# One hybrid decoder layer on one core: the cached-key products move to GpSimd, VectorE keeps one sum per page

## The reference, cut to what matters

```python
s_past = jnp.einsum('bthd,bshd->bhts', q, k_past) * scale
s_past = s_past + cq[..., None] + tail
p = softmax(concatenate([s_past, s_new]))
out = einsum('bhts,bshd->bthd', p[..., :P], v_past) + ...
```

## Time and profile before

| what | value |
|---|---|
| median of 3 runs | 1842.69 us (1839.71 to 1845.56) |
| profiled execution, from first to last instruction | 1838.9 us |
| TensorE busy | 1581.3 us (86%) |
| VectorE busy | 1037.4 us (56%) |
| ScalarE busy | 631.3 us (34%) |
| GpSimd busy | 242.0 us (13%) |
| mean granted TensorE clock | 0.908 |

### The profile page before, as it was taken

One profiled execution on the slowest core, in us unless ns is written; L12 is line 12 of the kernel. 1 busy time (PEld: TensorE's weight loads), 2 busy tenths in 40 slices (PEclk: granted clock), 3 DMA queues, 4 the chain that ended last, 5 costly groups with the idle time before them and its releaser, 6 DMA issues.

```text
span 1838.9 us, 33832 instructions
## 1 busy us (share of the span) xinstructions
PE 1581.3 (86%) x12263; PEld 1455.3 (79%) x12263; DVE 1037.4 (56%) x3203; ACT 631.3 (34%) x730; POOL 242.0 (13%) x379
## 2 busy tenths in 40 slices
PE   5999989783966667879777699999999999999996
PEld 4999868772743444569756699999999999999996
DVE  5557858567685887464663544444344444444444
ACT  5333313222241331333343344444233333333332
POOL 1000122121212222212103300000000000000332
PEclk9999989886977757789878799999999999999998
DMA  7456899886968688564342244554455554554553
GB/s 271 175 190 246 328 348 402 335 347 211 324 201 314 205 299 287 205 258 182 115 138 76 93 179 180 182 181 175 141 178 189 192 180 179 181 181 141 180 181 117
DMA packets 88612, 390.28 MB, mean 212 GB/s; under 512 B 9144, under 2 KB 22208, under 8 KB 66640
## 3 DMA queue, kind: packets, MB, share of 16 engines
q1 hardware_dynamic: 39824, 233.98, 35.4%
q0 software_dynamic: 39376, 143.15, 21.4%
q10 hardware_dynamic: 9328, 12.13, 1.9%
HBM read 379.13 MB, written 10.10 MB: 212 GB/s over the span
## 4 chain that ended last, share of the span: by engine, by line
PE 62%; DVE 14%; DMA 5%; issue 4%; ACT 2%; POOLq 1%; POOL 0%; DVEq 0%; ACTq 0%
PE bank L1388 18%; PE bank L1389 18%; PE bank L1390 18%; DVE page L933 4%; DMA page<-vc_dram 3%; DVE wlo L834 2%; DMA page<-kc_dram 2%; PE bank L1492 2%; ACT whi L492 1%; PE bank L1583 1%; DVE hl L873 1%; DMA g_s<-s_dram 1%; DMA nb<-mem_fm_dram 1%; DVE nb L888 1%; DVE g_dd L1099 0%
## 5 line engine op out<-in xcount | busy, mean ns | idle before, releaser
L1388 PE MATMUL bank<-hh,whi 128*128 128x264 f32 (+1 forms) x2688 | 779.3, 290 | 40.4 <-DVE hl L873 21.3
L1389 PE MATMUL bank<-hl,whi 128*128 128x264 f32 (+1 forms) x2688 | 770.9, 287 | 0.0
L1390 PE MATMUL bank<-hh,wlo 128*128 128x264 f32 (+1 forms) x2688 | 770.0, 286 | 0.0
L834 DVE TENSOR_TENSOR wlo<-raw,whi 128x2048 fp32r<-128x2048 f32 (+1 forms) x232 | 491.8, 2120 | 405.4 <-ACT whi L492 405.1
L492 ACT ACTIVATE whi<-raw 128x2048 fp32r<-128x2048 f32 (+1 forms) x232 | 410.4, 1769 | 837.8 <-PE bank L1390 833.7
L1388 PEld LDWEIGHTS bank<-hh,whi 128*128 128x128 f32 x2688 | 516.4, 192 | 55.0 <-issue 35.3
L1389 PEld LDWEIGHTS bank<-hl,whi 128*128 128x128 f32 x2688 | 517.0, 192 | 0.7 <-issue 0.7
L1390 PEld LDWEIGHTS bank<-hh,wlo 128*128 128x128 f32 x2688 | 514.1, 191 | 0.0
L933 DVE CUSTOM_DVE_ANT_0 page<-page,qb 128x128 f32<-128x128 f32 x1024 | 225.6, 285 | 70.8 <-DMA page<-kc_dram 52.4
L1388 PE MATMUL bank<-f_hi,whi 128*128 128x264 f32 x704 | 202.5, 288 | 7.5 <-DVE f_lo L1364 7.5
L1390 PE MATMUL bank<-f_hi,wlo 128*128 128x264 f32 x704 | 201.7, 287 | 0.0
(11 more groups left out here) (247 smaller groups left out, 1057.0 us busy)
## 6 DMA issues: line engine op xcount, KB each, us to landing
raw<-p_gu_dram SPq DMA_DIRECT2D x88, 1024.0 KB, 4.8
page<-kc_dram POOLq DMA_DIRECT2D x128, 512.0 KB, 6.2
page<-vc_dram POOLq DMA_DIRECT2D x128, 512.0 KB, 6.3
raw<-p_dn_dram SPq DMA_DIRECT2D x64, 704.0 KB, 4.1
raw<-p_fox_dram SPq DMA_DIRECT2D x24, 1024.0 KB, 4.8
raw<-p_gla_dram SPq DMA_DIRECT2D x24, 1024.0 KB, 7.7
raw<-p_out_dram SPq DMA_DIRECT2D x16, 1024.0 KB, 4.9
raw<-p_mem_dram SPq DMA_DIRECT2D x8, 1024.0 KB, 8.3
```

The source lines that it names most:

```text
L834: tt(wlo[:, k % 4, 0:blocks * P], raw[:, k % 4, 0:blocks * P], whi[:, k % 2, 0:blocks * P], ALU.subtract).then_inc(S("w_split"), 1)
L1388: mm(out, blk(whi, k % 2, b), rh, start=start, stop=False)
L1389: mm(out, blk(whi, k % 2, b), rl, start=False, stop=False)
L1390: return mm(out, blk(wlo, k, b), rh, start=False, stop=stop)
```

## The change

GpSimd now multiplies each key page in place with the query: `times_q` waits for the query and for the page, makes one `tensor_tensor` of 128x1024 and increments `k_mul`. It does so 7 items after it issued the page's load (`LAG`), ahead of the next fetch. The products of the last items of a turn thus come among the first fetches of the next. VectorE makes one `tensor_reduce` per page over all 8 heads (`k_sum`), one page later in its order than before, and frees the page with it. In the cross attention, `x_scores` becomes one product of 128x1024 and one sum, both on VectorE. `arrived` only moves.

```diff
@@ -359,6 +359,10 @@
             sp.wait_ge(S("y_out"), 64)
 
 
+        def arrived(t, q):
+
+            return 16 * (q // 8 + 1) if isinstance(t, int) and t == 0 else 64 * t - 32 + 16 * (q // 8 + 1)
+
         @block.gpsimd
         def _(pool):
             pool.dma_start(pts[:, :], io["pt_row"]).then_inc(S("pt_in"), 16)
@@ -374,10 +378,33 @@
                     pool.wait_ge(S(sem), value)
                 pool.dma_start(page[:, slot, :], io[src][ds(r * P, P), :]).then_inc(S(f"page_in{slot}"), 16)
 
+            LAG = 7
+
+            def times_q(t, j):
+
+                q = j if isinstance(t, int) and t == 0 else MIX.index(("k", j))
+                pg = page[:, q % SLOTS, :]
+                pool.wait_ge(S("q_b"), t + 1)
+                pool.wait_ge(S(f"page_in{q % SLOTS}"), arrived(t, q))
+                pool.tensor_tensor(pg, pg, qb[:, :], ALU.mult).then_inc(S("k_mul"), 1)
+
+            def times_before(t, q):
+
+                if q >= LAG:
+                    if MIX[q - LAG][0] == "k":
+                        times_q(t, MIX[q - LAG][1])
+                elif isinstance(t, int) and t == 1:
+                    times_q(0, 16 - LAG + q)
+                elif MIX[q + 32 - LAG][0] == "k":
+                    times_q(t - 1, MIX[q + 32 - LAG][1])
+
             pool.wait_ge(S("n_sq"), 4)
             for j in range(8):
+                if j >= LAG:
+                    times_q(0, j - LAG)
                 fetch("kc", j, j)
             for j in range(8, 16):
+                times_q(0, j - LAG)
                 fetch("kc", j, j - 8, "k_used", j - 7)
 
             def mixed(t, q):
@@ -393,11 +420,15 @@
                 fetch("kc" if now == "k" else "vc", 16 * t + j if now == "k" else 16 * t - 16 + j, q % SLOTS, sem, value)
 
             for q in range(32):
+                times_before(1, q)
                 mixed(1, q)
             with pool.Fori(2, 8) as t:
                 for q in range(32):
+                    times_before(t, q)
                     mixed(t, q)
             for j in range(16):
+                if j < LAG:
+                    times_before(8, j)
                 if j < SLOTS:
                     kind, i = MIX[32 - SLOTS + j]
                     fetch("vc", 112 + j, j, *(("k_used", 113 + i) if kind == "k" else ("v_used", 97 + i)))
@@ -437,10 +468,6 @@
                 cross_page(b)
             square_sums(3, "xo", "xo_go", 1)
             square_sums(4, "dn1", "n_lo_done", 16)
-
-        def arrived(t, q):
-
-            return 16 * (q // 8 + 1) if isinstance(t, int) and t == 0 else 64 * t - 32 + 16 * (q // 8 + 1)
 
         HN_BANKS = (2, 3, 6, 7)
 
@@ -923,19 +950,26 @@
 
             tail4 = tail[:, :].rearrange("p (h b j) -> p j b h", h=H, b=ND)
 
+            def k_slot(t, j):
+
+                q = j if isinstance(t, int) and t == 0 else MIX.index(("k", j))
+                return q, q % SLOTS
+
+            def k_sum(t, j):
+
+                _, slot = k_slot(t, j)
+                dve.wait_ge(S("k_mul"), 16 * t + j + 1)
+                dve.tensor_reduce(s_raw[:, j, :], page[:, slot, :].rearrange("p (h d) -> p h d", h=H), AX.X, ALU.add
+                                  ).then_inc(S("k_used"), 1)
+
             def k_page(t, j):
 
-                q = j if isinstance(t, int) and t == 0 else MIX.index(("k", j))
-                slot = q % SLOTS
-                dve.wait_ge(S(f"page_in{slot}"), arrived(t, q))
-                for h in range(H):
-                    pk = page[:, slot, P * h:P * h + P]
-                    ins = dve.tensor_tensor_reduce(out=pk, in0=pk, in1=qb[:, P * h:P * h + P], scale=1.0, scalar=0.0,
-                                                   op0=ALU.mult, op1=ALU.add, accum_out=s_raw[:, j, h:h + 1])
-                ins.then_inc(S("k_used"), 1)
+                if j:
+                    k_sum(t, j - 1)
 
             def s_max(t):
 
+                k_sum(t, PAGES - 1)
                 own("k_used", 16 * t + 16)
                 ch.link(tt(s_bias.rearrange("p (j b) h -> p j b h", b=1), s_raw.rearrange("p (j b) h -> p j b h", b=1),
                            tail4[:, :, ds(t, 1), :], ALU.add))
@@ -1267,12 +1301,11 @@
             def x_scores(b):
                 dve.wait_ge(S("xq_b"), b + 1)
                 dve.wait_ge(S(f"page_in{b}"), 16 * 33)
-                for m in range(2):
-                    for h in range(XH):
-                        pk = page[:, b, 512 * m + P * h:512 * m + P * h + P]
-                        ins = dve.tensor_tensor_reduce(out=pk, in0=pk, in1=x_qb[:, b % 2, P * h:P * h + P], scale=1.0, scalar=0.0,
-                                                       op0=ALU.mult, op1=ALU.add, accum_out=x_s[:, b, m, h:h + 1])
-                ins.then_inc(S("xk_used"), 1)
+                tt(page[:, b, :].rearrange("p (m n) -> p m n", m=2), page[:, b, :].rearrange("p (m n) -> p m n", m=2),
+                   row(x_qb[:, b % 2, :]).broadcast_to([P, 2, 512]), ALU.mult).then_inc(S("xk_mul"), 1)
+                own("xk_mul", b + 1)
+                dve.tensor_reduce(x_s[:, b, :, :].rearrange("p m h -> p (m h)"),
+                                  page[:, b, :].rearrange("p (m d) -> p m d", m=2 * XH), AX.X, ALU.add).then_inc(S("xk_used"), 1)
 
             f_start(0, False)
             f_start(1, False)
```

## The result

| what | before | after |
|---|---|---|
| median of 3 runs | 1842.69 us | 1997.23 us (1994.12 to 2000.58) |
| ratio, 95% interval | | 1.0848 [1.0823, 1.0873] |
| profiled execution, first to last instruction | 1838.9 us | 1992.4 us |
| mean granted TensorE clock | 0.908 | 0.884 |
| VectorE busy, GpSimd busy | 1037.4, 242.0 us | 1094.1, 557.0 us |

The account below looks back on a forecast made before the run. Latency sets the pace, VectorE in first halves of turns and GpSimd's loads in second halves; turns 1 to 7, turn 0 (+1) and cross attention (+6) together add 56 us to 1842.7, about 1900 us, range 1825 to 1960.

Parts of the forecast that it names:

- GpSimd's product: GpSimd's in-place multiplication of a 1024-element key page takes 2.5 us, bounds 2.03 and 2.93; 40 us of new work a turn.
- a pair of pages, first half of a gla turn: Two products, one split and about 0.5 us of loads after each other take 7.7 us, against 6.2 before; four pairs 31 us.
- a triple, second half: In a turn's second half, two value loads, a key load and its product cost GpSimd 5.5 us, against 3.7 before.
- wait at the end of a turn: After a turn's last product, a sum, the query copy and semaphores make the next product wait 3 us.
- run-ahead of the sequencer: GpSimd's sequencer prepares the next load beside a running product, so a first-half key page costs GpSimd 2.5 + 0.53 = 3.0 us.
- rival A: GpSimd's sequencer stands still during a product, so a first-half key page costs 3.7 us; 1944 us in all, chance 0.25.
- Rival B: GpSimd's product takes only 2.03 us, so VectorE's relief decides and the kernel gets faster, 1819 us; chance 0.14.
- rival C: No difference: the new work falls where GpSimd waits now and VectorE's relief pays for the rest, 1843 us; chance 0.08.
- Whoever is later waits: When GpSimd's products and VectorE's two-operand work meet, the later one waits; a gla pair then takes 7.7 us.
- stretched up to 4.5: Sign that the forecast is right: VectorE's splits of 2.3 us lengthen to as much as 4.5 us.
- about as much is lost to two-operand pieces: In a head turn's first half, pieces meeting products lose about the 4 us that VectorE's shorter pages save; it stays 32 us.
- hides most: Turn 4 (97 us) covers most new work behind the memory norm and its loads; +4 us (0 to 8).

## Why the prediction was right in kind and wrong in size

| step of the prediction | forecast | measured |
|---|---|---|
| VectorE's sum | 1.22 us | 1.21 us |
| GpSimd's product | 2.5 us (2.03 to 2.93) | 2.4 us undisturbed |
| load after a product | at once | at once (352.30; the product's recorded end is 352.36) |
| one-operand sums run free | yes | yes, 1.21 us throughout |
| a pair of pages, first half of a gla turn | 7.7 us | 10.4 us |
| first half, gla and head turn | 31 and 32 us | 43.4 (turn 2) and 41.1 us (turn 5, to the load at 649.43) |
| a triple, second half | 5.5 us | 6.0 to 6.4 us, once 8.1 |
| second half, eight triples | 44 us | 48.4 us (turn 2), 46.5 us (turn 5, from the load at 651.88) |
| wait at the end of a turn | 3 us | 2.6 us, 2.0 us |
| turns 1 to 7 | +49 us | +152 us |
| turn 0, cross attention | +1, +6 us | +4, +3.8 us (alone) |

**What held.** The price of the product was taken as the middle of two bounds, 2.5 us, and the run shows 2.35 to 2.41. The Trainium skill's figure in "GPSIMD Engine Reference", section "3.1 Elementwise — side-by-side cycle accounting", had given the estimate of 2.25 us, and the trace lies between the two. The run-ahead of the sequencer held, so rival A's mechanism is wrong (1944 us was nearer, but by another road): a load follows a product at once. That agrees with the Trainium skill, "GPSIMD Engine Reference", section "2.1 Instruction dispatch", by which instructions are pushed to a queue. Rival B fell with the product's length and rival C with the turns, which have no idle place for 40 us of products. The forecast's own range is narrower than its sum: by its 28 us for 0.25 us a product, the bounds of the product make 1847 to 1948 us and not 1865 to 1935; the result lies above both.

**The step that failed** is in the part on the two engines: "Whoever is later waits", and from it "In the first half of a gla turn a pair of pages then needs two products, one split and about 0.5 us of loads after each other: 2 x 2.5 + 2.2 + 0.5 = 7.7 us". That adds up only if the sums and the small pieces lie beside a product, as they would if the split got in after one. The rows show the split behind both products, the earlier of them recorded after it, and so the sums behind both as well, and GpSimd idle until the first is made: two products with their loads (0.6 + 5.35 us, from 319.03 to 324.98), the split's 2.16, two small pieces, the sum, and the way to the next load, in all 10.4. Its own sign, splits "stretched up to 4.5", was passed at 7.68 us. The first half makes 43.4 us instead of 31. In the head turns the same happens to scans, copies and products of `head_turn`, where the prediction had written "about as much is lost to two-operand pieces": 41.1 instead of 32, both from the end of the query copy to the load that the eighth page frees. At 9 to 12 us in each turn but turn 4, some 64 us, this one term is the larger part of the missing 103 us. That the split's wait follows the number of products in a row is shown by three runs (two products: 7.68; four: 12.67; one, when GpSimd waits for its own: 4.97), and that it is the cause in turns 1 to 3 by the splits that take an operand from PSUM: there the first half is back at about the forecast's 31 us (-35 us in all). In the head turns no run freed the pieces; there the cause is read from the timeline and not shown.

**The second step, smaller:** "in the second half two values and a key cost 2 x 1.24 + 2.5 + 0.53 = 5.5 us". With 8 slots and a lag of 7, the second load behind a product takes the slot of the page just multiplied, and waits 1.37 us for its sum, where the forecast had the usual 0.71 between loads. The wait on `k_used` was in the diff; the forecast followed it only to the end of the turn. It makes 2.5 to 4.4 us in the two turns of the table and 7 in turn 3. With lag 4 this wait is gone, and turns 5 to 7 are 7 to 9 us shorter, both halves together.

**The third:** turn 4 "hides most", +4 (0 to 8); it came out at +14. Of its six splits only one is stretched (3.23 us); the 16 `hl` pieces (line 900) of its first half take 17.7 us in all where they took 0.48 each before. The first half is 8 us longer and the rest 6; no run shows what lengthens the rest.

None of the changed kernels tried beats the kernel before; the nearest is the one that leaves the products out.

## What to carry to other kernels

Before work is given to GpSimd beside a VectorE that streams through SBUF, count the wait of a meeting as all the GpSimd products that follow each other closely (up to four here), not as one, and then follow who waits behind the VectorE operation; where that is GpSimd itself, both engines' work adds up instead of lying side by side. Removing one stretched operation can move the wait to the next, so such a cost is tested by taking the cause (here the product) away or halving it. And in a ring of loads, check for each load which work frees its slot: a lag one less than the ring makes a load wait for the operation just issued.

## What the runs showed of the hardware that was not expected

- VectorE is kept out through a run of GpSimd operations. A split of 2.28 us took 12.67 us across four products with loads between them; gaps of about 0.6 us, in which only a load's 0.59 us ran, didn't let it in. Why it got in after the fourth, ahead of a fifth that was as near, no run here shows; what keeps it out in the gaps isn't shown either. A load by itself didn't: in the kernel before, splits that began beside one took their 2.28 to 2.29 us. The Trainium skill, "SBUF — State Buffer", section "SBUF: two separate sides", says that whichever starts first holds the shared port pair "for the whole instruction" and that the other blocks. The runs agree on the blocking and show it lasting over several instructions. They do not show the order by recorded starts: the split of 319.46 waited for a product recorded 0.17 us after it, and with a lag of 4 a product recorded at 329.27 took 4.63 us while a split recorded at 329.40 took its 2.27.
- The products wait too: the one recorded at 142.26 in the changed kernel, 1.01 us after a split, took 3.50 us.
- Small operations of VectorE wait as well: a copy of 128x4 took 2.86 us in turn 5 of the changed kernel, and 11.56 with a lag of 4. The sums (`TENSOR_REDUCE`, 1.21 us in all 128 places) and a split with an operand in PSUM (2.28 us) never waited.
- The first load after a product takes 0.59 us instead of 0.53; two in a row there take 1.13 us together (lag 4, at 662.14), where two loads without a product start 1.24 us apart. A wait of GpSimd for its own product delays the next load by 1.31 us.
- The cost of the product grows faster than its length: 52 us for the first half, 101 for the second.
